# Long convolution by odd-frequency transforms with folded mirror pairs and a half-size inverse, in a fused two-block layer

## What is computed

```python
def _hyena_spectrum(length, ...):
    ...
    kern = jnp.concatenate([h[:, 0], jnp.zeros((1, D_HYENA), f32), h[:0:-1, 1]], axis=0)
    kern = kern * lax.rsqrt(jnp.sum(kern * kern, axis=0, keepdims=True) + EPS)
    return jnp.fft.rfft(kern, axis=0)

def _long_conv(u, spec, bias):
    length = u.shape[1]
    y = jnp.fft.irfft(jnp.fft.rfft(uf, n=2 * length, axis=1) * spec, n=2 * length, axis=1)[:, :length]
    return (y + uf * bias).astype(u.dtype)

def _hyena_gate_conv(u, spec, bias):
    x0, x1, v = jnp.split(u, 3, axis=-1)
    return x0 * _long_conv(x1 * v, spec, bias)
```

## Time and profile before

| | |
|---|---|
| runs of the kernel before | 1676.18, 1675.67, 1678.92 us; median 1676.18 |
| the profiled execution's own time | 1673.9 us |
| its span in the trace | 1672.1 us, 20787 instructions |
| mean granted TensorE clock | 0.997 of full |
| TensorE busy, weight loads | 1640.3 us (98%), 1305.9 us (78%) |
| VectorE, ScalarE, GpSimd busy | 845.3, 623.6, 647.7 us |

### The profile page before, as it was taken

How to read it: one execution, slowest core, us unless ns; L and a number is a source line. 1 busy time by engine, 2 the same in 40 slices (tenths; PEclk the granted TensorE clock), 3 DMA queues, 4 the chain that set the end, 5 groups by cost and what they waited for, 6 DMA issues and landing times.

```text
span 1672.1 us, 20787 instructions
## 1 busy us (share of the span) xinstructions
PE 1640.3 (98%) x8321; PEld 1305.9 (78%) x8321; DVE 845.3 (51%) x1206; ACT 623.6 (37%) x1007; POOL 647.7 (39%) x290
## 2 busy tenths in 40 slices
PE   7999999999999999999999999999999999999997
PEld 6876667788976777778877877887877888888886
DVE  5436685674134533333355645555657774343524
ACT  7534345654333532222323442643333322222223
POOL 4432222355731443334433333232244344444441
PEclk9999999999999999999999999999999999999998
DMA  7322211343620577743332234121134333333331
GB/s 229 106 76 65 64 51 57 95 123 110 189 83 13 176 231 263 262 152 96 96 122 84 74 92 148 51 76 38 38 115 138 86 91 101 100 91 99 101 92 59
DMA packets 295874, 181.22 MB, mean 108 GB/s; under 512 B 8465, under 2 KB 279603, under 8 KB 295524
## 3 DMA queue, kind: packets, MB, share of 16 engines
q1 hardware_dynamic: 291388, 170.50, 34.0%
q10 hardware_dynamic: 3832, 7.29, 1.3%
q0 software_dynamic: 560, 2.12, 0.4%
HBM read 174.09 MB, written 5.79 MB: 108 GB/s over the span
## 4 chain that ended last, share of the span: by engine, by line
PE 93%; DVE 3%; ACT 2%; issue 1%; DMA 0%; POOL 0%; SPq 0%; ACTq 0%; DVEq 0%
PE ps L1122 64%; PE ps L1134 13%; PE ps L1148 5%; PE ps L1471 1%; PE ps L1415 1%; PE ps L1396 1%; PE ps L1309 1%; PE ps L1283 1%; PE ps L1212 1%; PE ps L1295 1%; PE ps L1662 1%; PE ps L1332 1%; PE ps L1318 1%; DMA raw<-in_w_in_dram 0%; ACT WH L581 0%
## 5 line engine op out<-in xcount | busy, mean ns | idle before, releaser
L558 POOL TENSOR_TENSOR WL<-raw,WH 128x1024 fp32r<-128x1024 f32 (+2 forms) x282 | 645.2, 2290 | 989.3 <-ACT WH L581 989.1
L581 ACT ACTIVATE WH<-raw 128x1024 fp32r<-128x1024 f32 (+2 forms) x282 | 281.8, 1000 | 780.3 <-PE ps L1122 661.7
L1122 PE MATMUL ps<-hH,WH 128*128 128x512 f32 (+1 forms) x800 | 201.5, 394 | 0.0
L1122 PE MATMUL ps<-hL,WH 128*128 128x512 f32 (+1 forms) x800 | 197.8, 389 | 0.0
L1122 PE MATMUL ps<-hH,WL 128*128 128x512 f32 (+1 forms) x800 | 197.7, 389 | 0.0
L1122 PEld LDWEIGHTS ps<-hH,WH 128*128 128x128 f32 (+1 forms) x800 | 147.3, 187 | 37.4 <-issue 6.4
L1122 PEld LDWEIGHTS ps<-hL,WH 128*128 128x128 f32 (+1 forms) x800 | 149.5, 187 | 32.3
L1122 PEld LDWEIGHTS ps<-hH,WL 128*128 128x128 f32 (+1 forms) x800 | 149.5, 187 | 31.8
L1134 PE MATMUL ps<-hH,WH 128*128 128x512 f32 x328 | 136.9, 417 | 0.7 <-DVE vfTc L2176 0.7
L1134 PE MATMUL ps<-hH,WL 128*128 128x512 f32 x328 | 128.7, 392 | 0.0
L1134 PE MATMUL ps<-hL,WH 128*128 128x512 f32 x328 | 128.3, 391 | 0.0
(11 more groups left out here) (483 smaller groups left out, 2615.4 us busy)
## 6 DMA issues: line engine op xcount, KB each, us to landing
raw<-in_w_in_dram SPq DMA_DIRECT2D x64, 512.0 KB, 3.7
raw<-in_w_mlp_dram SPq DMA_DIRECT2D x64, 512.0 KB, 3.9
ada_w<-in_w_ada_dram SPq DMA_DIRECT2D x48, 512.0 KB, 5.7
raw<-in_w_gate_up_dram SPq DMA_DIRECT2D x44, 512.0 KB, 5.8
raw<-in_w_out_dram SPq DMA_DIRECT2D x16, 512.0 KB, 3.8
raw<-in_w_ckv_dram SPq DMA_DIRECT2D x16, 512.0 KB, 3.8
raw<-in_w_down_dram SPq DMA_DIRECT2D x16, 448.0 KB, 3.5
raw<-in_k_dft_dram SPq DMA_DIRECT2D x17, 256.0 KB, 2.7
```

The source lines that it names most:

```text
L558: pool.tensor_tensor(WL[un.slot][:, 0:s_.kt, 0:n], raw[un.slot][:, 0:s_.kt, 0:n], WH[un.slot][:, 0:s_.kt, 0:n].bitcast(F32), ALU.subtract) ...
L581: act.activation(WH[un.slot][:, 0:s_.kt, 0:n], raw[un.slot][:, 0:s_.kt, 0:n], ACT.Copy).then_inc(high_done, 1)
L1122: ins = pe.matmul(dst, w[un.slot][:, q, 0:m], a[:, q, :], start=(k == 0), stop=(k == 3 * kt - 1))
```

## The change

Four things are done at once.

1. *Odd frequencies.* The tables are now those of a transform at odd frequencies, angle pi (2f + 1) t / 1024 for t below 512. The first 256 columns are the frequencies 1, 3, ..., 511, the next 256 their mirrors 1023, 1021, ..., 513. No frequency needs a row of its own: the fifth "sa" unit, `nyq`, its product and copies, and the memset of a row of `spec` go. 
2. *Folding.* The mirrors of frequency tiles 0 and 1 are tiles 2 and 3. A pair (k, k + 2) is folded by VectorE, sum and difference of the two imaginary results and of the two real ones. The folded eight tiles serve two half-size inverses: one for even tokens, one for odd ones. Stage "inv" has 2 units of 8 tiles of weights, each weight set of 4 tiles making one bank: 2 x 2 x 4 x 3 = 48 matmuls. In product k = 2, 3 the results stay in their banks and the folds write banks; ScalarE rounds YH from banks and VectorE's low parts read banks.
3. *Order.* Transforms 2 and 6 come ahead of 1 and 5, and hyp tile 3, the last tile of the gate, stands between 1, 5 and 3, 7. The transforms take banks 5, 6, 3, 4, 2, 7, 0, 1 in turn, and the last two are the banks of the hyp tiles.
4. *The end.* The fillers ahead of the inverse go. The inverse does pair 0's 24 matmuls, then pair 1's 24 in four groups as the low parts come. The first projection unit's GLA half (12 matmuls) is put before the transposes, the second's behind them. VectorE evicts two banks per unit. Tokens come out even ones first, so the scaling reads the transposed bank in an interleaved order. ScalarE rounds the GLA tiles at the step where transform 3 ends.

The diff, without its parts on unused names and arguments:

```diff
-WEAVE = ([("hyp", i) for i in HYP_FIRST] + [("uu", 0), ("uu", 4), ("hyp", 2), ("uu", 1), ("uu", 5), ("hyp", 3)]
-         + [("uu", i) for i in (2, 6, 3, 7)])
+WEAVE = ([("hyp", i) for i in HYP_FIRST] + [("uu", 0), ("uu", 4), ("hyp", 2), ("uu", 2), ("uu", 6), ("uu", 1), ("uu", 5), ("hyp", 3)]
+         + [("uu", i) for i in (3, 7)])
+PAIRS = 2
...
-            Stage("sa", 5, 4, columns(t["k_dft"], kt=4)),
+            Stage("sa", 4, 4, columns(t["k_dft"], kt=4)),
...
-            Stage("uu", 8, 4, columns(t["k_dft"], kt=4), (5, 6, 3, 4)),
-            Stage("inv", 4, 8, columns(t["k_inv"])),
+            Stage("uu", 8, 4, columns(t["k_dft"], kt=4), (5, 6, 3, 4, 2, 7, 0, 1)),
+            Stage("inv", 2, 8, lambda i: t["k_inv"][i], (5, 6)),
...
+        def folded(k):
+            return ((at["uu", HT + k].bank, at["uu", HT + k + 2].bank), (at["uu", k].bank, at["uu", k + 2].bank))
...
-            keep_spec(at["sa", 4], nyq[:], 1)
...
-                act.wait_ge(bank_free, at["uu", HT + k].out + 1)
-                if k == 0:
-                    act.wait_ge(y_t, 1)
-                act.activation(YH[:, k, :], tmp[2 * (k % 2)][:], ACT.Copy)
-                act.activation(YH[:, HT + k, :], tmp[2 * (k % 2) + 1][:], ACT.Copy).then_inc(y_h, 1)
+                for c, (banks, places) in enumerate(zip(folded(k), ((k, 4 + k), (2 + k, 6 + k)))):
+                    act.wait_ge(y_t, PAIRS * k + c + 1)
+                    for b, q in zip(banks, places):
+                        act.activation(YH[:, q, :], bank(b), ACT.Copy).then_inc(y_h, 1)
...
-                if s_ - 1 in PAIR_STEP:
-                    high_Y(PAIR_STEP.index(s_ - 1))
-            high_Y(HT - 1)
-            act.wait_ge(gh_y, G_HEADS)
-            for k in range(HT):
-                act.activation(yH[:, HT + k, :], og[:, k, :], ACT.Copy).then_inc(og_h, 1)
+                if un is at["uu", 1]:
+                    high_Y(0)
+                if un is at["uu", 3]:
+                    act.wait_ge(gh_y, G_HEADS)
+                    for k in range(HT):
+                        act.activation(yH[:, HT + k, :], og[:, k, :], ACT.Copy).then_inc(og_h, 1)
+            high_Y(1)
...
+                    if un.bank == 2:
+                        pe.wait_ge(gh_scaled, G_HEADS)
+                    if un.bank == 7:
+                        pe.wait_ge(gh_y, G_HEADS)
...
-            pe.wait_ge(gh_scaled, G_HEADS)
-            keep_busy(2, 5)
-            after_opening("inv", YH, YL, [(k + 1 if not j else 0, HT * j + k) for k in range(HT) for j in range(2)], y_l, 2)
+            def inverse(e, q, c):
+                un = at["inv", e]
+                for j, b in enumerate((5 + e, 3 + e)):
+                    for n, (w, a) in enumerate(((WH, YH), (WH, YL), (WL, YH))):
+                        ins = pe.matmul(bank(b), w[un.slot][:, 4 * j + q, :], a[:, 4 * e + q, :],
+                                        start=(c == 0 and n == 0), stop=(c == 3 and n == 2))
+                if c == 3:
+                    ins.then_inc(unit_done, 1)
+            pe.wait_ge(y_l, 2 * PAIRS)
+            for e in range(2):
+                begin(at["inv", e])
+                inverse(e, 0, 0)
+                inverse(e, 2, 1)
+            for n, (e, q, c) in enumerate(((0, 1, 2), (1, 1, 2), (0, 3, 3), (1, 3, 3))):
+                pe.wait_ge(y_l, 2 * PAIRS + n + 1)
+                inverse(e, q, c)
+            wo = [at["wo", i] for i in range(2)]
+            def attention_half(un):
+                begin(un)
+                for c in range(HT):
+                    pe.wait_ge(y2_ok, c + 1)
+                    piece(un, yH, yL, [HT + c], c, DT)
+            attention_half(wo[0])
...
-            after_opening("wo", yH, yL, [(k + 1, (k + HT) % DT) for k in range(DT)], y2_ok, 2)
+            attention_half(wo[1])
+            for c in range(HT):
+                pe.wait_ge(y2_ok, HT + c + 1)
+                for un in wo:
+                    piece(un, yH, yL, [c], HT + c, DT)
+            units("wo", yH, yL, S, 2)
...
-            dve.wait_ge(bank_free, at["sb", 3].out + 1)
-            dve.memset(spec[0:1, HT, :], 0.0)
...
-            def low_Y(k):
-                dve.wait_ge(y_h, k + 1)
-                for j in range(2):
-                    ins = rest(tmp[2 * (k % 2) + j][:], YH[:, HT * j + k, :], YL[:, HT * j + k, :])
-                ins.then_inc(y_l, 1)
+            def low_Y(k, n):
+                b = (folded(k)[0] + folded(k)[1])[n]
+                q = (0, 4, 2, 6)[n] + k
+                dve.wait_ge(y_h, 4 * k + n + 1)
+                rest(bank(b), YH[:, q, :], YL[:, q, :]).then_inc(y_l, 1)
...
-                re, im = tmp[2 * (k % 2)], tmp[2 * (k % 2) + 1]
+                re, im = (tmp[2], tmp[3]) if k >= 2 else (tmp[0], tmp[1])
...
-                if k >= 2:
-                    dve.wait_ge(y_l, k - 1)
...
-                if k == 0:
-                    own.mark(dve.tensor_tensor(nyq[:], us[0:1, :], nyq[:], ALU.mult))
                 own.step(dve.tensor_tensor(im[:], us, kr, ALU.mult))
-                own.mark(dve.tensor_tensor(us, us, ks, ALU.mult))
-                own.settle()
-                dve.tensor_tensor(re[:], re[:], us, ALU.subtract).then_inc(bank_free, 1)
-                dve.tensor_tensor(im[:], ur, im[:], ALU.add).then_inc(bank_free, 1)
+                own.step(dve.tensor_tensor(us, us, ks, ALU.mult))
+                dve.tensor_tensor(us if k >= 2 else re[:], re[:], us, ALU.subtract).then_inc(bank_free, 1)
+                if k >= 2:
+                    taken(re_un)
+                    fold(k - 2, 0)
+                dve.tensor_tensor(ur if k >= 2 else im[:], ur, im[:], ALU.add).then_inc(bank_free, 1)
                 taken(im_un)
-                if k == 0:
-                    dve.tensor_copy(im[0:1, :], nyq[:]).then_inc(y_t, 1)
-                    dve.wait_ge(y_t, 1)
+                if k >= 2:
+                    fold(k - 2, 1)
+            def fold(k, c):
+                b, b2 = (bank(n) for n in folded(k)[c])
+                own.step(dve.tensor_tensor(b, tmp[c][:], b2, ALU.subtract if c else ALU.add))
+                dve.tensor_tensor(b2, tmp[c][:], b2, ALU.add if c else ALU.subtract).then_inc(y_t, 1)
+                dve.wait_ge(y_t, PAIRS * k + c + 1)
...
-                if s_ - 1 in PAIR_STEP:
-                    low_Y(PAIR_STEP.index(s_ - 1))
+                if un is at["uu", 1]:
+                    for n in range(2 * PAIRS):
+                        low_Y(0, n)
                 if s_ in PAIR_STEP:
                     product(PAIR_STEP.index(s_))
-            low_Y(HT - 1)
-            dve.wait_ge(y_l, HT)
-            def take(un, dst, m=P):
-                dve.wait_ge(unit_done, un.u + 1)
-                dve.tensor_copy(dst, bank(un.bank, S, m)).then_inc(bank_free, 1)
+            for n in range(2 * PAIRS):
+                low_Y(1, n)
+            dve.wait_ge(y_l, 4 * PAIRS)
...
-            for i in range(4):
-                take(at["inv", i], yt[:, i, :])
+            for e in range(2):
+                dve.wait_ge(unit_done, at["inv", e].u + 1)
+                dve.tensor_copy(yt[:, 2 * e, :], bank(5 + e))
+                dve.tensor_copy(yt[:, 2 * e + 1, :], bank(3 + e)).then_inc(bank_free, 1)
             dve.wait_ge(nrm_r, 1)
+            def by_token(a):
+                return a.rearrange("p (j m e) -> p j m e", j=2, e=2)
...
-                own.step(dve.scalar_tensor_tensor(tmp[1][:], bank(3 + c), nrm[:, c:c + 1], tmp[0][:], ALU.mult, ALU.add))
+                own.step(dve.scalar_tensor_tensor(by_token(tmp[1][:]), bank(3 + c).rearrange("p (e j m) -> p j m e", e=2, j=2),
+                                                  nrm[:, c:c + 1], by_token(tmp[0][:]), ALU.mult, ALU.add))
...
-    tt, ff = np.arange(S), np.arange(S)
-    turn = 2 * np.pi * ((tt[:, None] * ff[None, :]) % (2 * S)) / (2 * S)
+    tt = np.arange(S)
+    low_f = 2 * np.arange(S // 2) + 1
+    ff = np.concatenate([low_f, 2 * S - low_f])
+    turn = 2 * np.pi * ((tt[:, None] * ff[None, :]) % (4 * S)) / (4 * S)
     cos_m, sin_m = np.cos(turn), np.sin(turn)
-    alt = (-1.0) ** tt
-    sin_f = sin_m.copy()
-    sin_f[:, 0] = alt
-    dft = np.concatenate([cos_m, sin_f], axis=1)
-    cos_i, sin_i = cos_m / S, sin_m / S
-    cos_i[0] = 1 / (2 * S)
-    sin_i[0] = alt / (2 * S)
-    inverse = np.concatenate([cos_i, sin_i], axis=0)
+    dft = np.concatenate([cos_m, sin_m], axis=1)
+    inverse = np.zeros((2, P, 8, P))
+    for e in range(2):
+        for j in range(2):
+            some = tt[256 * j + e:256 * (j + 1):2]
+            for q in range(4):
+                inverse[e, :, 4 * j + q, :] = (sin_m if q > 1 else cos_m)[some, q % 2 * P:(q % 2 + 1) * P].T / S
```

5 lines of the change are left out of this document (2 added, 3 removed).

## The result

| | before | after |
|---|---|---|
| median of the runs | 1676.29 us (1675.67 to 1678.92, 4 runs) | 1666.15 us (1663.74 to 1666.81, 4 runs) |
| the profiled execution | 1673.9 us, span 1672.1 | 1666.81 us, span 1665.0 |
| mean granted TensorE clock | 0.997 | 0.995 |

Ratio after to before 0.9934, interval 0.9917 to 0.9951: 11 us less (8 to 14) by the ratio, 10.1 by the medians. The forecast was 1662.8 (1659.5 to 1667.0). So stages are compared here by the distance between two rows of one trace. That execution of before is also the fastest of all that are on record for it (28 more beside the experiments took 1674.16 to 1679.36 us).

The account below looks back on a forecast made before the run. TensorE, 98% busy, bounds the kernel, but VectorE's chain ends the inverse stage. Terms -2.72 and -10.65 give -13.4 us: 1660.5 on the profiled execution, plus 2.3 for the median, 1662.8 us; range 1659.5 to 1667.0.

Parts of the forecast that it names:

- Filter stage, -2.72: Filter stage: removing the fifth unit's 12 matmuls at 0.227 us saves 2.72 us; bounds 0 and -2.9.
- the POOL wait: Filter stage, ahead of the projection: TensorE's 1.10 us wait for POOL stays, 2.7 us earlier.
- the filter stage gives nothing: Filter stage: TensorE then waits for a chain of DVE or a slab; only -10.65, 1665.5 us; 7%.
- Unit 7's stall: Forward transforms: unit 7 waits for VectorE's taps of hyp tile 3, a new 0.8 us stall; bounds 0 and 3.
- the wait for the first low part: Inverse, after pair 0's 24 matmuls: TensorE waits 1.3 us for VectorE's low part, in place of 1.35.
- The rival with a worse backlog: Before unit 7: folds at twice the price give stall 3 and tail 2.8, some +4.5 us, 1667.3; 4%.
- The end of the stage, -10.65: Projection's opening: VectorE's chain, its product ending 0.5 us after POOL's two slabs, comes 10.65 us earlier.
- The interleaved scaling: VectorE's chain in the projection's opening: scaling priced at 0.75 us like the taps; high bound 2.9 us, four times.
- the rival with a slow one: Projection's opening: scaling at 1.5 us each, or a longer chain, +3 us, 1665.8; at high bound 1671.4; 12%.
- both clock rivals: TensorE's clock falls in the sparse projection opening: staying low, about 1717 us, 2%; low only there, 1668.2 us, 3%.
- the forecast's own case: Whole kernel: the summed terms hold, from -12 to -15 us; 72%.

Follow-up runs that it names:

- the ring experiment: The changed kernel with stage sb's banks taken in the order 1, 2, 0 instead of 0, 1, 2; 1663.79 us, ratio 0.9925.

## Why the prediction held, and where it was off

**Filter stage, -2.72: the step that failed.** It got 1.13. The unit's price was right and so was the POOL wait (1.09, forecast to stay). What I left out is which units become neighbours: each of the two stages counts through its own ring of three banks from bank 0, so the sine units keep theirs, but the first one now follows directly on a cosine unit with the same bank. The row of the new wait names ScalarE's copy of the bank; the ring experiment put the term at 2.71. I listed "the filter stage gives nothing" with DVE or a slab as its cause; the true cause was a third. (The prediction says that TensorE waits once between 970 and 1007 us. It also waits 1.36 us for ScalarE ahead of the transposes at 979.54, in both kernels alike.)

**Transforms and waits.** Unit 7's stall was forecast at 0.8 us and is 0.88 (1.04 by the starts: unit 3 is out at 1229.39, unit 7 starts at 1230.43); the wait for the first low part at 1.3 and is 1.19. The folds cost 0.69 to 0.70 us each, the low parts from banks 2.48 us for four. By the old trace's clock (2.54 us earlier) the second half starts at 1237.48, forecast 1237.2; the inverse is out at 1243.06, forecast 1242.7. The rival with a worse backlog did not come. Its sum was off besides: product 2 has four fold operations, not eight, so twice their price adds 2.8 us there and not 5.6.

**The end of the stage, -10.65: right in mechanism, 0.5 us too large.** The product under POOL ended at 1251.09, on the old clock 1248.55 for 1248.0 forecast. Two slabs took 4.92 us, ended at 1250.55 (1248.01 against my 1247.5), and the product 0.54 behind them, as the earlier trace rows had it. The chain behind the product was as before, three columns 2.63 us apart.

**The interleaved scaling.** Four times 0.75 us: the rival with a slow one falls, and the price taken from the taps was right.

**The clock.** No slice of the stage fell in the changed kernel, through waits of 0.82 to 1.19 us; both clock rivals fall as stated. But the clock was not free elsewhere. With hyp tile 3 ahead of transforms 1 and 5 it fell behind a 2.05 us wait. In unchanged code it fell behind the 1.2 us wait for attention tiles in five of the eleven profiles that have that wait, each time for 1.55 us or so. The Trainium skill, "TensorE: Matmul & The Clock Gate", section "A second HAM failure mode: psum-queue depth-cycling" (the prediction names the section ahead of it), tells of a kernel in which frequent short idles between groups of matmuls moved the clock between its two levels. In the stage where I weighed that, waits of 0.82 to 1.19 us cost nothing. Elsewhere the clock fell behind single waits of 1.21 and 2.05 us, and in two profiles among the small matmuls of the token sums near 1298 us, where the longest wait just ahead is 0.17 us.

**The total.** 1666.15 - 1662.8 = 3.4 us too low. The time lies inside the stated range, but the forecast's own case, "from -12 to -15 us" at 72%, did not come: it is 10.1 us less. The number lies near the first rival's (1665.5, 7%), and the range holds it only because it was drawn to take in the rivals. For the filter term, whose cause the rival did not have, that is luck. Of the 3.4 us, 1.6 is the bank (2.72 - 1.13) and 0.5 the stage. The 1.3 left fits the clock in untouched code: runs of the changed kernel at a mean clock of 0.998 took 1663.74, 1664.09 and 1664.75, those at 0.995 or less 1665.57 to 1666.81, two groups about 2 us apart, which is what the two dips (1.55 and 0.5 in the first profile) are worth. That is an inference, and it leaves something open. The 28 runs of before beside the experiments don't split that way: five at 0.998 took 1676.12 to 1676.39, and of seven at 0.995 six took 1675.88 to 1676.17. Over the twelve measurements that have a profile of both stages the gain of the medians lies between 2.5 us less and 1.1 us more than the gain that the rows of the two stages show, so 1.3 us is no more than what stays unexplained elsewhere. And the forecast had already carried over the 2.3 us by which the median of before lies above its profiled execution, which has neither dip and the earliest start of all. The kernel before has one profile, so how often its runs meet the dips is not known.

## What to carry to other kernels

When a unit leaves a sequence that rotates over banks, write the bank of each unit around the gap beside the old one before pricing its removal: two neighbours on the same bank cost 1.59 of 2.72 us here. When a stage is shortened, ask which other engine's work now falls beside the chain. Here GpSimd's slabs kept their length while everything around them moved, and four of the experiments were decided by which VectorE instruction lay under them.

## What was not expected of the hardware

- The operand's place decides whether VectorE waits for GpSimd: the same product beside a busy POOL took 1.98 us with both inputs in SBUF and 0.69 with one in a bank. A scaling with a bank as input ran at 0.75 to 0.76 in every case.
- Eleven profiles have the 1.2 us wait for the attention tiles. TensorE came out of it at 1151.86, 1152.01, 1152.21, 1152.50 and 1154.04 in the five in which the clock then fell, and at 1150.08 to 1151.55 in the six in which it did not. The length of the wait is the same, 1.21 or 1.22. It looks as if its place in time decides; why was not found. The ring's times need no such jump: worth 1.59 us in its stage, it moved the distance to before on the same chip from 10.14 to 11.76 us (the bare medians, 1666.15 and 1663.79, are of two chips).
- The start of the kernel alone moves the first landmark (the transposes of the filter stage) between 979.54 and 982.10 us over 13 profiles, with the same code ahead of it.
